# Pooling mixer: the channel scale moved from the mixed output into the pooling weights

## What is computed

```python
D_MODEL, SEQ, N_POOL_GROUPS, POOL_WINDOWS, POOL_GROUP_DIM = 1024, 256, 4, (2, 4, 8, 16), 256

def pool_mixer(h, w, b, scale):
    hg = h.reshape(bsz, s, N_POOL_GROUPS, POOL_GROUP_DIM)
    ...                                    # pooled[g]: mean of the last POOL_WINDOWS[g] tokens
    pooled = jnp.stack(pooled, axis=2).astype(h.dtype) - hg
    mixed = jnp.einsum('bsgc,gcd->bsgd', pooled, w) + b
    return mixed.reshape(bsz, s, D_MODEL) * scale

x = x + pool_mixer(rms_norm(x, norm_mix[0]), pool_w[0], pool_b[0], pool_scale[0])
h = rms_norm(x, norm_ffn[0])
x = x + swiglu(h, ffn_w1[0], ffn_w3[0], ffn_w2[0])   # 1024 -> 3584 -> 1024
...                                                  # K/V, attention, experts, final norm
```

## Time and profile before

| | us |
|---|---|
| median of 3 runs | 1246.3 |
| lowest, highest | 1245.36, 1246.53 |
| the profiled execution, its own time | 1245.78 |
| its span, from the first to the last instruction | 1244.0 |
| TensorE busy in the span | 1215.7 |
| VectorE, ScalarE, GpSimd busy | 285.3, 201.5, 48.7 |
| mean granted TensorE clock | 0.997 of full |

### The profile page before, as it was taken

The page is one execution under the profiler, slowest core; times in us unless marked ns, Lnnn a source line. Parts: engine busy times, 40 slices in busy tenths (PEclk is TensorE's granted clock), DMA queues, the critical chain, the costliest instruction groups (busy, mean ns, idle before and its releaser), DMA issues.

```text
span 1244.0 us, 28356 instructions
## 1 busy us (share of the span) xinstructions
PE 1215.7 (98%) x13440; PEld 774.4 (62%) x13440; DVE 285.3 (23%) x374; ACT 201.5 (16%) x280; POOL 48.7 (4%) x45
## 2 busy tenths in 40 slices
PE   7999999999999999999999999999999999999995
PEld 6888888888743473377568447755743664474464
DVE  4555454468541100110110011011001101100122
ACT  4443434365520000000000000000000000000001
POOL 4000000011010000000000000000000000000000
PEclk9999999999999999999999999999999999999998
DMA  9965556423499999999999999999999999999970
GB/s 346 391 239 196 184 189 202 136 89 123 144 356 406 407 409 419 402 411 412 409 408 412 412 407 411 412 410 408 410 412 409 410 407 418 406 417 411 413 316 37
DMA packets 101469, 423.47 MB, mean 340 GB/s; under 512 B 9074, under 2 KB 17956, under 8 KB 101348
## 3 DMA queue, kind: packets, MB, share of 16 engines
q1 hardware_dynamic: 94288, 410.59, 83.9%
q0 software_dynamic: 2240, 7.09, 1.6%
q10 hardware_dynamic: 4820, 3.93, 1.0%
HBM read 416.72 MB, written 4.85 MB: 339 GB/s over the span
## 4 chain that ended last, share of the span: by engine, by line
PE 97%; DVE 1%; ACT 1%; issue 1%; DMA 0%; ACTq 0%; DVEq 0%
PE psum L736 46%; PE psum L747 24%; PE psum L648 8%; PE psum L650 7%; PE psum L649 7%; PE psum L717 0%; PE psum L656 0%; PE psum L941 0%; PE psum L918 0%; DMA consts<-in_table 0%; PE psum L827 0%; PE psum L887 0%; PE psum L928 0%; DVE x_res L1518 0%; PE psum L1043 0%
## 5 line engine op out<-in xcount | busy, mean ns | idle before, releaser
L736 PE MATMUL psum<-up,xg 128*32 128x448 f32 x6144 | 580.4, 539 | 0.6 <-DVE xg L1734 0.6
L736 PEld LDWEIGHTS psum<-up,xg 128*32 128x32 f32 x6144 | 251.9, 110 | 323.6 <-issue 321.9
L747 PE MATMUL psum<-down,hid_t 128*32 128x256 f32 x5376 | 296.7, 379 | 4.0 <-issue 3.8
L747 PEld LDWEIGHTS psum<-down,hid_t 128*32 128x32 f32 x5376 | 235.7, 110 | 65.4 <-issue 12.2
L1489 DVE TENSOR_TENSOR sil<-sil,psum 128x1344 f32<-128x1344 f32 x16 | 24.9, 1554 | 761.2 <-PE psum L736 761.2
L1365 DVE TENSOR_TENSOR low<-raw,high 128x2048 fp32r<-128x2048 f32 x50 | 114.6, 2291 | 86.0 <-ACT high L1080 85.8
L1080 ACT ACTIVATE high<-raw 128x2048 fp32r<-128x2048 f32 x51 | 97.8, 1918 | 82.5 <-PE psum L650 81.2
L648 PE MATMUL psum<-high,a_hi 128*128 128x512 f32 x224 | 87.3, 390 | 0.9 <-DVE a_lo L1402 0.9
L650 PE MATMUL psum<-low,a_hi 128*128 128x512 f32 x224 | 87.2, 389 | 0.0
L649 PE MATMUL psum<-high,a_lo 128*128 128x512 f32 x224 | 87.2, 389 | 0.0
L1160 ACT ACTIVATE sil<-psum 128x1344 f32<-128x1344 f32 x16 | 20.7, 1291 | 409.0 <-PE psum L736 409.0
(11 more groups left out here) (219 smaller groups left out, 567.2 us busy)
## 6 DMA issues: line engine op xcount, KB each, us to landing
up<-in_moe_w SPq DMA_DIRECT2D x256, 896.0 KB, 8.7
down<-in_moe_w SPq DMA_DIRECT2D x112, 1024.0 KB, 8.4
raw<-in_ffn_w SPq DMA_DIRECT2D x42, 1024.0 KB, 5.7
raw<-in_w_q SPq DMA_DIRECT2D x4, 1024.0 KB, 5.1
raw<-in_w_o SPq DMA_DIRECT2D x4, 1024.0 KB, 4.9
y_rows<-y_sb ACTq DMA_DIRECT2D x28, 96.0 KB, 9.2
x_res<-in_x SPq DMA_DIRECT2D x2, 512.0 KB, 4.4
raw<-in_pool_w SPq DMA_DIRECT2D x1, 1024.0 KB, 10.2
```

The costliest lines, as they stand in the source:

```text
L736: mm = pe.matmul(out3[g * BLK:(g + 1) * BLK, r, :], xg[:, k, r * BLK:(r + 1) * BLK], w[:, g], start=k == 0, stop=k == DT - 1)
L747: mm = pe.matmul(Y[g * BLK:(g + 1) * BLK, r, :], hid_t[:, c, r, b * BLK:(b + 1) * BLK], w[:, bb, g * GW:(g + 1) * GW], start=c == 0 and b ...
```

## The change

DVE no longer multiplies the mixed banks by the scale. Instead it multiplies the pooling weights in place, by columns. The scale comes as one row on one partition (`scale_row`, a 4 KB load on ACT's queue), is spread over the 128 partitions by two matmuls against a row of ones, into the banks of `OUT[1]` (6 and 7), and DVE reads it there. The mixed banks are then added straight to the stream, a half at a time. Two runs of `keep_warm` get shorter, and the small transpose goes to bank 5, since bank 7 now holds the scale. The spread copy of the scale in `pool_rows` is still loaded, for the bias on POOL.

```diff
+        scale_row = at("scale_row", [1, D], F32, o_b + 12 * K)
...
             pe.wait_ge(consts_in, 16)
-            keep_warm(0, 12)
+            keep_warm(0, 4)
+            pe.wait_ge(scale_in, 16)
+            for half in range(2):
+                pe.matmul(banks[OUT[1][half]][:], consts[0:1, C_ONE:C_ONE + P], scale_row[:, half * CW:(half + 1) * CW],
+                          start=True, stop=True).then_inc(scale_spread, 1)
             pe.wait_ge(xn_ready, NT)
...
                     pe.wait_ge(vec_in, 16 * 7)
-                    pe.transpose(banks[7][:, 0:NV], vec_rows[:, :], ident[0:NV, 0:NV]).then_inc(vec_turned, 1)
+                    pe.transpose(banks[5][:, 0:NV], vec_rows[:, :], ident[0:NV, 0:NV]).then_inc(vec_turned, 1)
...
                         pe.wait_ge(pooled_odd if g % 2 else pooled_even, g // 2 + 1)
+                        pe.wait_ge(w_scaled, g // 2 + 1)
...
             turn_tile(x_res, x_ready, 0, 0, bank=2)
-            keep_warm(0, 5)
+            keep_warm(0, 1)
             turn_tile(x_res, x_ready, 0, 1, bank=2)
...
             act.dma_start(consts[:, 0:C_COS], table[:, 0:C_COS]).then_inc(consts_in, 16)
+            act.dma_start(scale_row[:], pool_scale).then_inc(scale_in, 16)
...
             for b in (0, 2):
...
                 mm.then_inc(pooled_even, 1)
-            dve.wait_ge(pool_in, 32)
+                h = b // 2
+                w = raw[U_POOLW][:, h * 1024:(h + 1) * 1024].rearrange("p (g k f) -> p g k f", g=2, k=2)
+                scale = banks[OUT[1][h]].rearrange("p (g f) -> p g f", g=2).unsqueeze(2).to_broadcast([P, 2, 2, 256])
+                dve.wait_ge(scale_spread, h + 1)
+                dve.wait_ge(landed[U_POOLW], 16)
+                dve.tensor_tensor(w, w, scale, ALU.mult).then_inc(w_scaled, 1)
             for t in range(NT):
                 dve.wait_ge(mixed, t + 1)
+                dve.wait_ge(pool_ready, t + 1)
                 for half in range(2):
                     s = slice(half * CW, (half + 1) * CW)
-                    mm = dve.tensor_tensor(xn[:, t, s], banks[OUT[t][half]][:], pool_rows[:, 1, s], ALU.mult)
-                step(mm)
-                dve.wait_ge(pool_ready, t + 1)
-                dve.tensor_tensor(x_res[:, t, :], x_res[:, t, :], xn[:, t, :], ALU.add).then_inc(x_ready, 1)
+                    mm = dve.tensor_tensor(x_res[:, t, s], x_res[:, t, s], banks[OUT[t][half]][:], ALU.add)
+                mm.then_inc(x_ready, 1)
```

## The result

The changed kernel takes 1250.97 us (median of 8 runs, 1248.71 to 1251.95) against 1246.39 of the kernel before (8 runs, 1245.36 to 1246.77), a ratio of 1.0037 with a 95% interval of 1.0028 to 1.0047. It is 4.6 us slower, where 2.7 us faster was forecast, and its runs spread over 3.2 us where those of before spread over 1.4. The profiled execution has a span of 1248.7 us.

The account below looks back on a forecast made before the run. TensorE, 97% of the chain, was taken as the bound. The adds' 2.87 us less 0.2 for scaling gave 2.67 earlier: 1245.78 - 2.67 = 1243.1, the median 0.5 above, about 1243.6 us; range 1242.5 to 1245.7.

Parts of the forecast that it names:

- All behind the first dense matmul moves with it: From the first dense matmul, at 29.00 us before, to the end: the program shifts one to one with that matmul's start.
- The adds, 2.87 us: Between mixing and second transposes: adds reading a bank are not held up by GpSimd's split, so transposes start 2.87 us earlier.
- no room: Between mixing and second transposes: the old keep_warm's remaining 8 instructions would not fit and would have cost 1.0 us.
- The weights' scaling, 0.2 us: DVE scaling the pooling weights before mixing: 1.2 us each, making mixing wait at the third weight group; cost 0.2 us.
- The spreading, 0 us: TensorE before the band matmuls: two 512-column matmuls replace eight of 128, so the bands start where they did; cost 0 us.
- Rival 1: Opening: one-row spreading or idling leaves TensorE's clock low into band and mixing matmuls; 2 us lost, 1245.4 us; 12 in 100.
- Rival 2: After mixing: shorter keep_warm lets the clock fall, 4.0 us of dense work at half speed, 1245.6 us; 6 in 100.
- Rival 3: Before the band matmuls: the scale row's load lands late and TensorE waits, up to 1251.5 us; 9 in 100.

Follow-up runs that it names:

- zero-row version: The changed kernel with the scale's row in a 128-row tile, other rows zeroed by VectorE, the load issued behind that; 1235.88 us against 1238.66 for the kernel before.
- the row of ones: The changed kernel with the spread row replaced by ones from the constants, all 128 rows used, no load; 1236.19 us against 1238.66 for the kernel before.
- ScalarE's copy: The changed kernel without spreading matmuls or 4 KB load, first warming 12 long, ScalarE copying the scale into the banks; 1236.21 us against 1238.66 for the kernel before.
- one-row version: The kernel before with 8 of its first 12 warming matmuls replaced by two of 512 columns using one array row; 1243.78 us against 1238.31.
- 128-row one: The kernel before with 8 of its first 12 warming matmuls replaced by two of 512 columns using all 128 rows; 1238.16 us against 1238.31.
- with nothing ahead of them: The kernel before without its first run of warming matmuls, so the band matmuls come first; 1242.30 us against 1238.79.
- the version with the 512 KB load: The changed kernel with the scale spread by its 512 KB load on ScalarE's queue, copied to banks by 128-row matmuls; 1241.98 us against 1238.31 for the kernel before.

## Why the prediction was wrong

- **All behind the first dense matmul moves with it: right.** Span less start of the first dense matmul is 1215.0 and 1215.4 on the first chip, and 1207.0 to 1207.8 in all ten profiled runs on the others, over starts from 26.4 to 34.8.
- **The adds, 2.87 us: right.** They take 1.28 or 1.29 us a pair beside GpSimd's split too. By itself the step gave 2.6 us between medians, and its interval holds the 2.87. In that trace the turn from the end of mixing to the second transposes takes 24.59 - 23.21 = 1.38 us; 1.44 had been reckoned. That there was "no room" for more warming in it was right as well: in the zero-row version the chain runs through TensorE's own transposes and the short `keep_warm`, which end within 0.1 us of the adds.
- **The weights' scaling, 0.2 us: right.** First scaling forecast at 14.3 for 1.2 us, seen at 14.30 for 1.22; mixing forecast to start at 15.6, seen at 15.67; its wait at the third group forecast as 0.2, seen as 7.33 - 7.17 = 0.16; first dense matmul forecast at 26.3, seen at 26.36. These are from the trace of the zero-row version. In the versions with the row of ones and with ScalarE's copy mixing starts later, at 16.71 and 15.83, and takes 7.17 and 7.18: no wait. In the changed kernel the slow bands hid the scaling altogether. One argument of this step was weaker than it looked: the pair of pooled banks at 11.57, taken as the case without GpSimd, had GpSimd's product of bias and scale beside it (from 11.25 for 2.34 us).
- **The spreading, 0 us: this step failed.** It said: "1024 columns for 1024. [...] If duration follows columns [...] the band matmuls start where they did". Duration does nearly follow columns (3.71 us for the one-row version, 3.41 for the 128-row one, both at 1.2 GHz). But the step asked only how long the matmuls take, and not what they do to the clock: it put at nothing the loss of the 128-row work behind which the clock had risen. What the runs show in its place is a clock that stays at 1.2 GHz until 23.65, against 8.89. Measured, one row in place of 128 costs 1243.78 - 1238.16 = 5.6 us in the kernel before. Between the two versions of the change, one 4.3 us over the kernel before and the other 2.8 under, it is 7.1 us.
- **Rival 1 held the cause, with 12 in 100 and a quarter of the price.** "The spreading matmuls use one row of the array" was the mechanism. I priced it as a loss of 2 us by taking it that the clock, begun anew, would rise 4.0 us into the band matmuls. They took 6.3 us for it with nothing ahead of them, and 7.7 and 10.1 us in the traces of the changed kernel run again and of the one-row version. In the changed kernel on the first chip 11.2 us of them did not do it, and the clock rose 1.6 us into mixing. With 1.2 us for the later start of the bands, 5.2 for the bands and 0.8 for mixing, it would have read 1243.6 + 7.2 = 1250.8, slower. The band matmuls had never been seen on a low clock, and I took a duration from one trace of the warming matmuls, a different kind of work. Even for those 4.0 us was one case of several: in the six versions in which warming matmuls, or 128-row ones of 512 columns behind them, run without a gap up to the bands, the rise came 3.2 to 6.1 us after the first of them. The bound asked for was the whole stage at half speed.
- **Rival 2: did not occur.** In the traces of all kernels with the shorter second `keep_warm` the granted clock does not fall behind mixing, and the dense matmuls follow the second transposes by 1.97 or 1.98 us, as before. The rule on transposes from the Trainium skill, "TensorE: Matmul & The Clock Gate", section "Part 4: PE-mode transpose", that in that mode they do not count as busy, cost nothing here. Whether transposes alone would hold the clock for longer no run here shows.
- **Rival 3: did not occur in the change**, where the spreading starts at 7.08, right behind the warming. It did in the version with the 512 KB load. Its worst case, a loss of 5.5 us, should have read 1246.3 + 5.5 = 1251.8 and not 1251.5.
